# Who makes the low parts of eight weight units while the state-space outputs are made

## The reference

```python
hn = rms_norm(h, norm1_g[l])
q, k, v, u, g_na, g_ssm = jnp.split(hn @ w_in[l], IN_SPLITS, axis=-1)
...
y_na = neighbourhood_attention(q, k, v, na_rpb[l]).reshape(b, L, NA_WIDTH) @ w_proj_na[l]
y_ssm = s5_branch(u, ssm_lam_re[l], ..., w_glu[l]) @ w_proj_ssm[l]
mixed = jax.nn.sigmoid(g_na) * y_na + jax.nn.sigmoid(g_ssm) * y_ssm
h = h + mixed @ w_out[l]
h = h + conv_gated_ffn(rms_norm(h, norm2_g[l]), w_up[l], conv_w[l], conv_b[l], w_down[l])
```

```python
bu = jnp.einsum('blgc,gnc->blgn', u.astype(jnp.complex64), b_bar)
a = jnp.broadcast_to(lam_bar, bu.shape)
_, states = lax.associative_scan(_ssm_combine, (a, bu), axis=1, reverse=reverse)
return jnp.real(jnp.einsum('blgn,gcn->blgc', states, c_mat))
```

## Time and profile before

| | |
|---|---|
| Runs of the kernel | 1491.43, 1491.97, 1492.33 us; median 1491.97 |
| Span of the profiled execution | 1488.4 us |
| TensorE busy | 1460.3 us (98%), mean granted clock 0.993 |
| VectorE, ScalarE, GpSimd busy | 593.9 us (40%), 672.6 us (45%), 1052.9 us (71%) |
| The stage of the change | from about 325 to 386 us of the span |

### The profile page before, as it was taken

How to read it: one execution, slowest core, us unless ns; L and a number is a source line. 1 busy time by engine, 2 the same in 40 slices (tenths; PEclk the granted TensorE clock), 3 DMA queues, 4 the chain that set the end, 5 groups by cost and what they waited for, 6 DMA issues and landing times.

```text
span 1488.4 us, 30666 instructions
## 1 busy us (share of the span) xinstructions
PE 1460.3 (98%) x11826; PEld 1387.4 (93%) x11826; DVE 593.9 (40%) x1151; ACT 672.6 (45%) x913; POOL 1052.9 (71%) x496
## 2 busy tenths in 40 slices
PE   8999999999999999999999999999999999999997
PEld 7999999998888899999999999999999998888886
DVE  3766788888556334443322222222222222003002
ACT  6446444431335464444554444444444443334333
POOL 5400038873578678888788888888888887888885
PEclk9999999999999999999999999999999999999999
DMA  7897457653576455575555565555555555555553
GB/s 221 288 223 216 134 159 220 197 177 93 153 229 210 152 169 170 183 257 178 177 185 184 183 184 183 183 183 182 181 182 181 182 182 197 193 185 184 191 189 129
DMA packets 250494, 277.14 MB, mean 186 GB/s; under 512 B 30748, under 2 KB 236924, under 8 KB 249772
## 3 DMA queue, kind: packets, MB, share of 16 engines
q1 hardware_dynamic: 235840, 254.84, 56.2%
q10 hardware_dynamic: 14508, 21.09, 4.3%
q0 software_dynamic: 64, 0.07, 0.0%
HBM read 263.32 MB, written 12.39 MB: 185 GB/s over the span
## 4 chain that ended last, share of the span: by engine, by line
PE 80%; DVE 10%; DVEq 2%; issue 2%; DMA 2%; ACT 2%; SPq 1%; POOL 0%; ACTq 0%
PE ps L1538 20%; PE ps L1540 20%; PE ps L1539 20%; PE ps L1907 6%; PE ps L1906 6%; PE ps L1908 6%; DVE ps L1065 3%; DVE scan_states L1254 3%; DVEq L1253 2%; DMA w_raw<-in_w_in 1%; PE ps L1748 1%; DVE t L1065 1%; SPq L462 1%; ACT w_hi L520 1%; DVE w_lo L524 1%
## 5 line engine op out<-in xcount | busy, mean ns | idle before, releaser
L524 POOL TENSOR_TENSOR w_lo<-w_raw,w_hi 128x1024 fp32r<-128x1024 f32 x425 | 1023.2, 2414 | 398.8 <-ACT w_hi L520 257.5
L520 ACT ACTIVATE w_hi<-w_raw 128x1024 fp32r<-128x1024 f32 x464 | 490.2, 1060 | 677.7 <-PE ps L1540 492.8
L1538 PE MATMUL ps<-act_hi,w_hi 128*128 128x258 f32 (+2 forms) x2432 | 696.4, 286 | 1.0 <-DVE act_lo L1006 1.0
L1540 PE MATMUL ps<-act_hi,w_lo 128*128 128x258 f32 (+2 forms) x2432 | 691.8, 284 | 0.0
L1539 PE MATMUL ps<-act_lo,w_hi 128*128 128x258 f32 (+2 forms) x2432 | 691.2, 284 | 0.0
L1538 PEld LDWEIGHTS ps<-act_hi,w_hi 128*128 128x128 f32 x2432 | 463.0, 190 | 6.1 <-issue 4.4
L1539 PEld LDWEIGHTS ps<-act_lo,w_hi 128*128 128x128 f32 x2432 | 463.4, 191 | 0.0
L1540 PEld LDWEIGHTS ps<-act_hi,w_lo 128*128 128x128 f32 x2432 | 462.0, 190 | 0.0
L1906 PE MATMUL ps<-w_hi,hidden_hi 128*128 128x512 f32 x352 | 139.2, 395 | 0.0
L1908 PE MATMUL ps<-w_lo,hidden_hi 128*128 128x512 f32 x352 | 139.0, 395 | 0.0
L1907 PE MATMUL ps<-w_hi,hidden_lo 128*128 128x512 f32 x352 | 139.0, 395 | 0.0
(11 more groups left out here) (268 smaller groups left out, 1563.3 us busy)
## 6 DMA issues: line engine op xcount, KB each, us to landing
w_raw<-in_w_up SPq DMA_DIRECT2D x176, 512.0 KB, 3.5
w_raw<-in_w_in SPq DMA_DIRECT2D x128, 512.0 KB, 4.1
w_raw<-in_w_down SPq DMA_DIRECT2D x88, 512.0 KB, 3.9
w_raw<-in_w_out SPq DMA_DIRECT2D x32, 512.0 KB, 3.4
w_raw<-in_w_proj_na SPq DMA_DIRECT2D x16, 512.0 KB, 3.4
w_raw<-in_w_proj_ssm SPq DMA_DIRECT2D x16, 512.0 KB, 3.3
w_raw<-in_w_glu SPq DMA_DIRECT2D x8, 512.0 KB, 3.5
bias_rows<-skew_scratch ACTq DMA_DIRECT2D x24, 128.0 KB
```

The source lines that it names most:

```text
L520: act.activation(slot(whi, k), slot(raw, k), ACT.Copy).then_inc(s_hi, 1)
L524: pool.tensor_tensor(slot(wlo, k), slot(raw, k), slot(whi, k).bitcast(F), ALU.subtract).then_inc(s_lo, 1)
L1538: mm(o, slot(whi, k)[:, cols], xh[:, kt, lo:lo + n], start=kt == 0, stop=False)
L1540: ins = mm(o, slot(wlo, k)[:, cols], xh[:, kt, lo:lo + n], start=False, stop=kt == units * UKT - 1)
```

## The change

The eight low parts of units 92 to 99 move from GpSimd's program to VectorE's, one at the head of each tile, ahead of `y_out(t)`. GpSimd first waits for `s_gm`, sets the meta bias to zero and makes `bias_reach(0)`, and then waits until VectorE has made all eight (`s_lo`). VectorE waits once, ahead of the loop, until GpSimd has made the low parts before them. Nothing moves on TensorE, ScalarE and SyncE.

```diff
-            for n in range(4 * G_SSM):
-                lo_unit(pool, U_G + DEPTH + 4 * G_SCAN, n)
-                if n == 6:
-                    pool.wait_ge(s_gm, KH)
-                    pool.memset(bm[:, :, 0:N_META], 0.0).then_inc(s_bz, 1)
-                    bias_reach(0)
+            pool.wait_ge(s_gm, KH)
+            pool.memset(bm[:, :, 0:N_META], 0.0).then_inc(s_bz, 1)
+            bias_reach(0)
+            pool.wait_ge(s_lo, U_G + DEPTH + 4 * G_SCAN + KH)
...
             g_make(1)
+            dve.wait_ge(s_lo, U_G + DEPTH + 4 * G_SCAN)
             for t in range(KH):
+                lo_unit(dve, U_G + DEPTH + 4 * G_SCAN, t)
                 y_out(t)
```

## The result

The changed kernel takes 1483.13 us (median of 4 runs, 1481.69 to 1487.81) against 1491.85 us before (4 runs, 1491.43 to 1492.33). The ratio is 0.9947 with a 95% interval of 0.9933 to 0.9960: faster by 8.7 us, where 5.65 us were forecast. Two more measurements, on two chips, gave the ratios 0.9941 and 0.9945.

The account below looks back on a forecast made before the run. TensorE, busy 98% of the span, bounds the kernel. Savings of 1.09 + 2.16 + 1.52 = 4.77 us, with 0.88 at the first scores 5.65, take the span from 1488.4 to 1482.7 and the median to 1486.3 us; range 1484.6 to 1489.6.

Parts of the forecast that it names:

- VectorE's stretch: In g_make, VectorE rows stand still until GpSimd's subtraction is done: 2.13 us on one addition, 2.26 us on one product.
- the moved work is hidden: VectorE's loop with the added subtraction is 6.15 us inside TensorE's 7.10, so the addition costs nothing.
- the waits of 1.09 and 2.16 us: TensorE's waits for g_make at kernels of tiles 1 and 4; both forecast as saved, the second at worst 2.0.
- the remaining 1.08 us: TensorE's wait at chunk_out(7) for its strip, behind the gate scaling; no part is GpSimd's, so it stays.
- the first `scores`: Start of the attention stage: its 0.88 us wait for loads goes, as they land 6.9 us earlier.
- the attention stage: Later 3.2 us wait for loads: could shrink by 1.2 us or grow by up to 2.8; taken as 0.
- it gives back more: Rival: the attention stage's 3.2 us wait shrinks by 1.2, giving 1485.1 us; chance 7%.
- The half clock in tile 4: Fall of TensorE's clock behind the 2.16 us wait, taken as gone: 1.52 us saved.
- With the same distance: The median's 3.6 us above the profiled span is kept, turning the forecast span of 1482.7 into 1486.3 us.
- The half clock did come at another place: Rival: the half clock comes anyway elsewhere, for instance behind 382.30, giving 1487.8 us; chance 10%.
- the early weight load delays the bias loads: Rival in the attention stage: unit 103's early load takes back up to 2.8 us, giving 1489.1; chance 15%.
- VectorE as the bound: Rival: the stretch stays, VectorE's loop is 8.3 us against 7.10, giving 1499; decides above 0.95 us left; chance 6%.

Follow-up runs that it names:

- the delayed GpSimd: GpSimd keeps all eight subtractions of the kernel before, but starts each only once g_make(t+1) is finished; 1484.0 us, ratio 0.9954.
- the exchange: Changed kernel, with ScalarE's att_hi and att_load ahead of the block's first hi_unit from the third attention block on; 1480.94 us, ratio 0.9924.
- the holding of the loads: Changed kernel, with SyncE also waiting for chunk_out(6) before the first attention load; 1488.48 us, ratio 0.9973.
- the version with two tiles: Against the kernel before, only the subtractions of tiles 0 and 3 are made on VectorE, six stay on GpSimd; 1487.42 us, ratio 0.9971.
- the exchange on the kernel before: Kernel before, with ScalarE's att_hi and att_load ahead of the block's first hi_unit from the third attention block on; 1489.77 us, ratio 0.9987.
- both edits: Changed kernel, with the gate scaling of tile 6 behind strip_out(7) and ScalarE's att_hi and att_load ahead of hi_unit; 1482.71 us, ratio 0.9931.

## Why the prediction was right and wrong

**What held.** VectorE's stretch is GpSimd's subtraction (shown by the delayed GpSimd); the moved work is hidden; the waits of 1.09 and 2.16 us go; the remaining 1.08 us are the gate scaling's (shown by its move); the loads start 7.1 us earlier where 6.9 was forecast (371.88 and 372.1) and free the first `scores`, 1.0 us where 0.88 was taken. The profiled span was forecast as 1482.7 and was 1482.3. That near hit is partly luck: `chunk_out(7)` came 5.06 us earlier instead of 4.77 and the later waits shrank by 1.1, and in return this execution lost 1.7 us to a fall at 424 us; 0.7 us of the 6.1 between the two profiles are not accounted for. The warning of the Trainium skill, Perfetto Trace Analysis, section "Optimizing Scalar/DVE Operations", that moving work between these two engines might not help, would have given 1492. It doesn't decide where the two collide in time. The exclusive lock of the Trainium skill, SBUF — State Buffer, section "SBUF: two separate sides", does, and the trace agrees: 3.36 us became 1.24.

**The step that failed** is the attention stage: "I take 0, as SyncE's queue is gated again by GpSimd's subtractions". The later waits for loads fell from 2.7 to 1.4 us on average, as much as the rival "it gives back more" had named with 7%. What went wrong is the size of the gate's move. GpSimd's subtractions there did not come 5 to 6 us earlier but 6.5 and then 7.1 (the one of 417.79 at 410.74). So ScalarE's high part, behind which the loads stand, came 7.2 us earlier (428.02 and 420.81), and TensorE reached the fourth `scores` 6.0 earlier (430.67 and 424.66). The wait shrank by the difference, 3.19 to 2.07 us in these two profiles: the 1.2 us that the forecast had worked out and set to 0. That the wait hangs on ScalarE's order is shown by the exchange, and that it grows when SyncE's queue starts late by the holding of the loads. Why the weights of that high part are late in both kernels no run tested. With 1.3 us in place of this 0 the forecast would have been 1485.0, still 1.9 above the measured time, so the other terms count too.

**Two terms were too small.** The half clock in tile 4 was sized at 1.52 from one execution; over four it is 2.1. And the undisturbed tile period, 7.10 to 7.15 us before, is 7.06 to 7.09 after, where the forecast left it alone: with other small delays 0.3 us in the stage. Why is open. Sum of the corrections: 1.3 + 0.6 + 0.3 + 0.1 on 5.65 is 8.0, against 8.2 between mean spans and 8.7 between the medians. The last 0.7 us, and what makes 9.3 and 9.6 of it elsewhere, are within the spread of executions and stay open. The 1.3 is a reading of four profiles each; no pair of medians shows it by itself.

**The anchor.** "With the same distance" took the 3.6 us between span and median as fixed. It was 1.75 us around the span and 1.8 us by which that execution was better than its median, because it met fewer falls of the clock (from 320 us on 1.7 us lost where three others lost 5.1, over the whole span 8.5 where they lost 10 to 12). This left the sum alone, but it should have warned that the trace showed the clock's cost at its lowest, and that the range of 1.5 us below the forecast was too narrow.

**The rivals.** The half clock did come at another place, at 424 us, in half the profiles after, with 1.7 us; but the falls behind the stage cost before as much on average (1.7 us, once at 432 and three times at 544), so they took nothing of the gain. In the version with the held loads it took back a good part. That the early weight load delays the bias loads was not seen. VectorE as the bound was far off: its loop was 6.1 us of 7.09. Its point of decision was near in the version with two tiles, where one stretched row and one moved subtraction in a row were too much.

## What to carry to other kernels

Where VectorE and GpSimd work at one time, look for VectorE rows whose length jumps by the rest of a GpSimd row, and follow the first to TensorE; moving GpSimd's start behind them was worth nearly as much here as moving its work (7.9 against 9.6 us). A wait on TensorE can cost more than its length, by the clock behind it, and a single trace shows only one draw of that cost: set the profiled execution's own time against the runs before taking a size from it. A transfer whose start depends on the stage that gets faster gains its head start too, and a wait behind it is to be counted with the gain.

## What the hardware showed that was not expected

- The half clock came in pieces: a fall cost 1.7 us of lost work (windows of 8 us at a mean clock of 0.79), or twice that, at 352, 424 to 432 and 536 to 544 us, behind a wait of TensorE each time. The length of the wait doesn't settle it: 3.19 us at 433.86 was followed by none, 2.07 us at 426.73 by one.
- Matmuls of ones in a wait of 2.16 us kept the clock at 1.00; the kernel before gains 1.5 us by them (0.9979 to 1.0000) though the matmuls behind the wait start no earlier.
- A VectorE addition with both inputs in SBUF stood for up to 2.1 us behind a GpSimd subtraction (1.23 became 3.36). The rows of `y_out` and `strip_out`, which read one input from PSUM, were never stretched: with GpSimd delayed, seven groups of `y_out` and four rows of `strip_out` lie over a subtraction, wholly or in part, and keep their 0.87 and 0.38 us. In the kernel before only one strip row lies over one.
- It works the other way too: where the VectorE row began first, GpSimd's was the longer one, 2.90 us at 360.40 beside the addition of 359.78 and 2.84 at 327.80, where 2.40 is usual. This cost nothing, as GpSimd waited 4.9 and 5.4 us for ScalarE ahead of its next subtraction.
- In the profiles of three edited kernels (two tiles, the exchange on the kernel before, both edits) the wait for `w_tr` near 140 us was 2.5 to 2.6 us instead of 1.4 to 1.7, though no edit touches that stretch. Its cause is open.
